# Three blocks of a transformer on one core: in the first two attentions the outputs are scaled instead of the probabilities, and the work around them is dealt out anew

## The reference

```python
# layer 0, per block of 128 queries: 12 heads over the block and 128 keys on either side, and a sink
s = einsum('bqkgd,bskd->bkgqs', q_blk, k_blk) * scale + bias
p = softmax(concatenate([where(valid, s, NEG), sink_l], -1), -1)[..., :SPAN]
o = einsum('bkgqs,bskd->bqkgd', p, v_blk)
# layer 1, per row of a grid 64 wide: 12 heads over all 8 rows and 16 columns around the query
s = einsum('bwhd,brwchd->bhwrc', q_row, k_nb) * scale + bias
o = einsum('bhwrc,brwchd->bwhd', softmax(s), v_nb)
# both: 4 more heads over a memory of 256 tokens
o_mem = einsum('bhsm,bmhd->bshd', softmax(q @ mk * scale), mv)
x = x + rms_norm(concatenate([tok, mem_out], -1) @ w_out[i], g)
```

## Time and profile before

| | |
|---|---|
| time before, median of 3 | 1915.09 us (1914.83 to 1916.83) |
| profiled execution | 1917.37 us, of which the span of the core is 1915.6 us |
| granted clock over the span | 0.997 |
| busy: PE, DVE, ACT, POOL | 1897.8, 964.2, 772.1, 182.8 us |
| windowed phase, scores of turn 4 to the end | 93.57 to 154.74 us of the span |
| grid phase, the same | 681.65 to 739.93 us of the span |

### The profile page before, as it was taken

One profiled execution on the slowest core, in us unless ns is written; L12 is line 12 of the kernel. 1 busy time (PEld: TensorE's weight loads), 2 busy tenths in 40 slices (PEclk: granted clock), 3 DMA queues, 4 the chain that ended last, 5 costly groups with the idle time before them and its releaser, 6 DMA issues.

```text
span 1915.6 us, 25105 instructions
## 1 busy us (share of the span) xinstructions
PE 1897.8 (99%) x10458; PEld 1567.2 (82%) x10458; DVE 964.2 (50%) x1497; ACT 772.1 (40%) x1251; POOL 182.8 (10%) x196
## 2 busy tenths in 40 slices
PE   9999999999999999999999999999999999999998
PEld 7878888888888867888888888878887888888887
DVE  5693665553245284566553236443655555425523
ACT  5494433333333295433333334233764443212321
POOL 4112200000005031300000103000000020000000
PEclk9999999999999999999999999999999999999999
DMA  6512233334333311232233332331112323233222
GB/s 191 197 35 77 80 97 99 99 92 141 93 104 123 99 41 56 89 98 92 97 99 91 102 105 99 99 106 61 59 38 86 116 90 97 99 99 96 93 97 88
DMA packets 54136, 182.96 MB, mean 96 GB/s; under 512 B 6604, under 2 KB 10060, under 8 KB 53512
## 3 DMA queue, kind: packets, MB, share of 16 engines
q1 hardware_dynamic: 51528, 172.28, 28.2%
q0 software_dynamic: 2352, 9.02, 1.6%
q10 hardware_dynamic: 144, 0.06, 0.0%
HBM read 176.58 MB, written 4.76 MB: 95 GB/s over the span
## 4 chain that ended last, share of the span: by engine, by line
PE 88%; ACT 5%; DVE 5%; issue 1%; DMA 1%; SPq 0%; DVEq 0%; ACTq 0%
PE bank L1903 22%; PE bank L1904 22%; PE bank L1905 22%; PE bank L1922 2%; ACT prob_long L848 2%; PE bank L1923 2%; PE bank L1924 2%; ACT pt_short L837 1%; PE bank L2153 1%; PE bank L1683 1%; PE bank L1686 1%; PE bank L1691 1%; PE bank L1981 1%; PE bank L1982 1%; PE bank L1983 1%
## 5 line engine op out<-in xcount | busy, mean ns | idle before, releaser
L1155 DVE TENSOR_TENSOR w_lo<-w_raw,w_hi 128x1024 fp32r<-128x1024 f32 (+3 forms) x319 | 388.6, 1220 | 712.3 <-ACT w_hi L661 711.9
L661 ACT CAST w_hi<-w_raw 128x1024 fp32r<-128x1024 f32 (+3 forms) x319 | 322.0, 1010 | 555.0 <-DMA w_raw<-in_w_down 132.4
L1903 PE MATMUL bank<-h_hi,w_hi 128*128 128x512 f32 x1272 | 497.1, 391 | 0.8 <-DVE w_lo L1155 0.5
L1904 PE MATMUL bank<-h_lo,w_hi 128*128 128x512 f32 x1272 | 496.1, 390 | 0.0
L1905 PE MATMUL bank<-h_hi,w_lo 128*128 128x512 f32 x1272 | 495.9, 390 | 0.0
L1903 PEld LDWEIGHTS bank<-h_hi,w_hi 128*128 128x128 f32 x1272 | 239.5, 188 | 53.1 <-issue 2.2
L1905 PEld LDWEIGHTS bank<-h_hi,w_lo 128*128 128x128 f32 x1272 | 239.5, 188 | 50.2
L1904 PEld LDWEIGHTS bank<-h_lo,w_hi 128*128 128x128 f32 x1272 | 239.5, 188 | 49.5
L1903 PE MATMUL bank<-a_hi,w_hi 128*128 128x512 f32 (+1 forms) x676 | 261.5, 387 | 0.0
L1904 PE MATMUL bank<-a_lo,w_hi 128*128 128x512 f32 (+1 forms) x676 | 261.3, 387 | 0.0
L1905 PE MATMUL bank<-a_hi,w_lo 128*128 128x512 f32 (+1 forms) x676 | 261.3, 386 | 0.0
(11 more groups left out here) (328 smaller groups left out, 2551.6 us busy)
## 6 DMA issues: line engine op xcount, KB each, us to landing
w_raw<-in_w_gu SPq DMA_DIRECT2D x87, 512.0 KB, 3.5
w_raw<-in_w_mlp_in SPq DMA_DIRECT2D x32, 512.0 KB, 3.5
w_raw<-in_w_mlp_out SPq DMA_DIRECT2D x32, 512.0 KB, 3.6
w_raw<-in_w_down SPq DMA_DIRECT2D x32, 448.0 KB, 3.3
w_raw<-in_w_out SPq DMA_DIRECT2D x24, 512.0 KB, 3.6
w_raw<-in_w_down SPq DMA_DIRECT2D x16, 512.0 KB, 3.5
w_raw<-in_w_gates SPq DMA_DIRECT2D x16, 512.0 KB, 3.4
w_raw<-in_w_qk_b SPq DMA_DIRECT2D x14, 512.0 KB, 3.7
```

The source lines that it names most:

```text
L661: nc.scalar.copy(hi_of(v), raw_of(v)).then_inc(w_hi_done, 1)
L1155: nc.vector.tensor_tensor(lo_of(v), raw_of(v), hi_of(v).bitcast(F32), ALU.subtract).then_inc(w_split, 1)
L1903: mm(acc, w1, hi, start=start, stop=False)
L1904: mm(acc, w1, lo, start=False, stop=False)
```

## The change

- **Scaling.** VectorE no longer scales the probabilities. TensorE turns and multiplies the bare exponentials, and so waits for `p_exp` in place of `p_ready`. Once for each pair VectorE takes the reciprocals of all 8 sums and spreads them over 512 columns of `raw` (`spread_roots`); TensorE turns these in 8 more transposes beside those of the next pair's first step (or alone in turn 35), they are copied out with the same `copy_turned` (1024 columns in place of 512), and VectorE multiplies the pair's output by them (`scaled_output`), rounds it and later subtracts (`scaled_remainder`).
- **Skew.** ScalarE makes the exponentials of step `s-1` in turn `s`, no longer those of step `s`.
- **Dealing.** The output operations are VectorE's alone, in different turns of four: the spread in turns 4k+1, the copy of one step's turned probabilities (the pair's last, `by_vector`) in turns 4k+2, the subtraction in 4k+3, the product and rounding in 4k. ScalarE makes three of four copies and no `h_hi`.
- **Ring.** The values of the grid phase lie in a ring of tiles, so that each step reads two whole blocks of 128 key rows; 64 columns of `prob_long` that the first and last query tile don't use are set to zero at the start.
- **Order.** The first dense stage after the attention does seven chunks of its third tile first, and then the last chunks of the first three tiles.

```diff
@@ attention steps of the grid phase
-            spans = [(0, 192, 256, ((0, P), (64, P)), (0, 1), (slice(0, 64), slice(0, P))),
...
+            spans = [(0, 192, 256, 64, (0, 1)), (64, 256, 0, 0, (1, 2)), (192, 256, 0, 0, (2, 3)),
+                     (320, 192, 448, 0, (3, 0))]
@@
+        def turned_blocks(phase, d, steps):
+            begin, end = 0, 2 * len(steps[d].blocks) if d < len(steps) else 4
+            if phase < 2 and d and d % 4 == 0:
+                begin, end = 0 if d < len(steps) else 4, 8
+            return begin, end
+
+        def by_vector(phase, d, steps):
+            return phase < 2 and d < len(steps) and d % 4 == 3
@@ ScalarE, copy_turned and the turn
+                if by_vector(phase, d, steps):
+                    turned[0] += 1
+                    return
...
+                if phase < 2 and d % 4 == 2 and d > 2:
+                    act.wait_ge(o_scaled, scaled[0] + d // 4)
                 act.wait_ge(t_ready, turned[0] + 1)
...
-                        if s < n:
-                            exps(phase, s, steps[s])
-                        if 0 <= s - LAG_V[phase] < n:
-                            copy_output(phase, s - LAG_V[phase], steps, o_hi)
+                        if 0 <= s - 1 < n:
+                            exps(phase, s - 1, steps[s - 1])
@@ VectorE
+                def spread_roots(d):
+                    of = steps[d].pair_no % 2
+                    dve.wait_ge(p_exp, expd[0] + 2 * d + 2)
+                    nc.vector.reciprocal(rden[:, :, :], sums[:, :, :, of]).then_inc(rden_done, 1)
...
+                    nc.vector.tensor_copy(raw[:, of, :].rearrange("p (n d) -> p n d", n=8), spread).then_inc(roots_spread, 1)
+
+                def scaled_output(d):
...
+                    dve.wait_ge(pt_copied, turned[0] + d + 2)
+                    dve.wait_ge(pv_done, pv[0] + d + 1)
+                    nc.vector.tensor_tensor(o, acc, pt_of(phase, d + 1)[:, 4 * P:8 * P], ALU.mult).then_inc(o_scaled, 1)
+                    dve.wait_ge(o_scaled, o_count[0])
+                    nc.vector.tensor_copy(o_hi[:, st.pair, :], o).then_inc(o_hi_done, 1)
...
+                def copy_turned(d):
+                    dve.wait_ge(pv_done, pv[0] + d - 1)
+                    dve.wait_ge(t_ready, turned[0] + d + 1)
...
+                    nc.vector.tensor_copy(dst, src).then_inc(pt_copied, 1)
+
+                def beside_minima(s):
+                    if s >= 5 and s % 4 == 1 and s - 2 < n:
+                        spread_roots(s - 2)
+                    if s >= 8 and s % 4 == 0:
+                        scaled_output(s - 5)
+                        if s >= n:
+                            scaled_remainder(s - 5)
+                    if s >= 11 and s % 4 == 3 and s - 3 < n:
+                        scaled_remainder(s - 8)
+                    if s >= 6 and s % 4 == 2 and s - 3 < n:
+                        copy_turned(s - 3)
@@ VectorE's turn, after the minima of step s
-                        for half in range(2):
-                            part = prob_of(phase, d, half)[:, :steps[d].width]
-                            nc.vector.tensor_scalar(part, part, rden[:, i, half:half + 1], None, ALU.mult).then_inc(p_ready, 1)
...
+                        beside_minima(s)
@@ TensorE, turn
-                    pe.wait_ge(p_ready, ready[0])
+                    pe.wait_ge(p_exp if phase < 2 else p_ready, ready[0])
...
+                if phase < 2 and d and d % 4 == 0:
+                    pe.wait_ge(roots_spread, heads[0] + d // 4)
+                    for i in range(4):
+                        for part in range(2):
+                            last = nc.tensor.transpose(ps[4 + part][:, 256 + 64 * i:256 + 64 * i + 64],
+                                                       raw[rows(part), (d // 4 - 1) % 2, P * i:P * i + P],
+                                                       ident[rows(part), 64 * part:64 * part + 64])
```

More of the change, by code:

```diff
@@ L887, in softmax @@
                 pv[0] += n
-            masked, turned, pv = [0], [0], [0]
+                if phase < 2:
+                    scaled[0] += n // 4
+            masked, turned, pv, scaled = [0], [0], [0], [0]
             logs_and_exps()
@@ L1276, in softmax @@
                 n = len(steps)
+                for i, first in ((0, 0), (3, 192)) if phase == 1 else ():
+                    unused = prob_long[:, 2 * i:2 * i + 2, first:first + 64]
+                    nc.vector.tensor_copy(unused, zero_bias[:, :P].rearrange("p (h k) -> p h k", h=2)).then_inc(round_cleared, 1)
                 if last_values:
@@ L1670, in chunk_order @@
                              for c in range(m)]
+                    if st in w_out:
+                        plain = [(2, 0, c) for c in range(7)] + [(k, 0, 7) for k in range(3)] + plain[3 * DC:]
                     if st is w_out2:
@@ L2058, in turn @@
             def turn(phase, d, steps, act_read):
+                if d == 0 and phase == 1:
+                    pe.wait_ge(round_cleared, 2)
                 if d == 0:
                     wait_reads((act_read, 0, 0))
-                if not 0 <= d < len(steps):
+                if not (0 <= d < len(steps) or phase < 2 and d == len(steps)):
                     return
-                blocks = steps[d].blocks
                 if turned[0]:
                     pe.wait_ge(pt_copied, turned[0])
-                for half in range(2):
+                for half in range(2 if d < len(steps) else 0):
+                    blocks = steps[d].blocks
                     ready[0] += 1
-                    pe.wait_ge(p_ready, ready[0])
+                    pe.wait_ge(p_exp if phase < 2 else p_ready, ready[0])
                     first_key = steps[d].pieces[0][half]["first_key"]
@@ L2083, in softmax @@
                 n = len(steps)
+                if phase == 2:
+                    ready[0] = 0
                 if last_values:
@@ L2134, in softmax @@
                         pe.wait_ge(pt_copied, copied[0])
-                        banks = 1 if phase == 2 else 2
-                        if st.first and st.pair_no >= banks:
-                            pe.wait_ge(o_ready, heads[0] + st.pair_no - banks + 1)
+                        if st.first and phase < 2 and st.pair_no >= 2:
+                            pe.wait_ge(o_scaled, heads[0] + st.pair_no - 1)
+                        elif st.first and phase == 2 and st.pair_no:
+                            pe.wait_ge(o_ready, heads[0] + st.pair_no)
                         n_v = len(st.vs[0])
```

88 lines of the change are left out of this document (48 added, 40 removed).

## The result

| | before | after |
|---|---|---|
| median of 18 executions each | 1915.20 us (1913.61 to 1917.11) | 1920.12 us (1917.67 to 1923.61) |
| ratio | | 1.0023, interval 1.0016 to 1.0031 |
| profiled execution, span | 1917.37, 1915.6 us | 1917.97, 1916.2 us |
| windowed phase, scores of turn 4 to the last product with values | 61.17 us | 64.70 us |
| grid phase, the same | 58.28 us | 58.86 us |

The change makes the kernel slower, by 4.9 us between the medians. The two phases alone, both at full clock, differ by 3.53 + 0.58 = 4.1 us.

The account below looks back on a forecast made before the run. ScalarE and VectorE were nearly full, TensorE's own work within 3% of the bound in the windowed phase. Windowed +3.5 and grid -0.1 gave +3.4 us, so the median 1915.09 becomes 1918.5 us, range 1914.0 to 1922.0.

Parts of the forecast that it names:

- The windowed phase, +3.5: Windowed attention: old waits -3.1, eight transposes 8 x 0.26, new waits +4.2, turn 33 +0.3; sum +3.5 us.
- Wait (a): Turns 4k+2: TensorE waits for VectorE's copy behind both minima; with restart 0.37 us windowed, 0.43 grid, 0.33 at the memory.
- wait (b): Turns 4k+3: TensorE waits for ScalarE's copy of 1024 columns; with restart 0.18 us windowed, 0.28 grid.
- (c): Windowed phase: ScalarE's exponentials of 385 columns between two copies add 0.09 us a pair, between 0 and 0.2.
- The price of VectorE's copy: VectorE's copy of 512 float32 columns out of PSUM: taken as 0.68 us, with 0.42 as the other end.
- The rival of a short copy at 0.42: VectorE's copy takes 0.42 us; 14 waits fall by 0.26 each, -3.6, giving 1914.9, no change; chance 0.12.
- Eight transposes, 0.26: TensorE's eight added transposes for a pair cost 0.26 us on the path, 4.2 us over 16 pairs.
- The rival of hidden copies, -5.9: Copies are hidden and TensorE runs without waits: -5.9 us, giving 1909.2; chance 0.08.
- The grid phase, -0.1: Grid attention: -5.8 old waits, -1.8 64-row products, +2.1 transposes, +4.6 new waits, +0.3 turn 33, +0.5 GpSimd; sum -0.1 us.
- GpSimd's remainder: First grid pairs: VectorE's new operations meet GpSimd's masking and delay VectorE's copy; 0.5 us, ends 0 and 3.
- The rival at +3: GpSimd holds VectorE longer in the first three or four grid pairs: +3 in place of +0.5, giving 1921.0; chance 0.15.
- What was to cost nothing: Skew, VectorE's five new operations outside the priced waits, the last pair's output and the two clears: no cost claimed.

Follow-up runs that it names:

- e1: The changed kernel with VectorE's copy of turned probabilities put ahead of the two minima of its turn; 1913.15 us, ratio 0.9994.
- e5: The kernel before with GpSimd's mask copies for grid pairs 3 to 5 cut to 8 columns; 1912.79 us, ratio 0.9988.
- e6: Windowed attention in the order of the kernel before, grid attention as in e1; 1913.56 us, ratio 0.9994.
- e4: The changed kernel with GpSimd's masks of the bias tables of grid pairs 3 to 5 added on 8 columns only; 1919.17 us, ratio 1.0019.
- e8: e2 with the skew taken back, exponentials of step s in turn s again; 1915.03 us, ratio 0.9999.
- e2: The changed kernel with ScalarE making all four copies of a pair, VectorE none; 1914.97 us, ratio 1.0000.
- e3: The changed kernel without the 8 transposes of spread reciprocals in all turns but each phase's last; 1915.61 us, ratio 1.0004.
- e7: As e6, but ScalarE makes all four copies of a grid pair; 1913.10 us, ratio 0.9988.
- e9: The kernel before with the third block's 16 single-column products dealt one column at a time behind 8 projection chunks; 1913.61 us, ratio 0.9993.
- e10: e7 with the same edit as e9, narrow products dealt behind projection chunks; 1911.10 us, ratio 0.9978.

## Why the prediction was right, and where it was off

The forecast was 1918.5 us, in a range of 1914 to 1922; the runs gave 1920.12, inside. The chance for slower by over 0.2% was 0.40, that for no change 0.49, and the ratio, 1.0023, is just over the bound: what happened was not what the prediction held likeliest of the three. Of the 1.5 us between forecast and median, 0.7 is in the phases, all of it in the grid phase; the rest lies outside them. The direction, the place and the price were worked out before the run; by its steps:

- *The windowed phase, +3.5*: measured +3.53. Wait (a), forecast 0.37 with restart, measured 0.34; wait (b), forecast 0.18, measured 0.13; (c), forecast 0.09, measured 0.04 before one transpose and 0.05 before another. The period was forecast at 7.8 and is 7.87.
- *The price of VectorE's copy*, unknown from the trace of before: 0.68 was taken, 686 ns measured. The rival of a short copy at 0.42 falls. By the Trainium skill, "VectorE: DVE Perf Modes", section "Why PSUM operands drop a tier", a float32 operand in PSUM takes away VectorE's faster modes, and the estimate from that page was 0.66 us; this trace agrees with 0.686 (and with 0.427 for the copy of 512 columns that stays in SBUF).
- *Eight transposes, 0.26*: measured 0.27 by leaving them out.
- *The rival of hidden copies, -5.9*: did not come, and for the reason given: order, not load. Even e1, which takes the order away, comes, in the two phases, to 5.6 under the change and only 1.5 under the kernel before, as waits of 2.1 and 2.8 remain.
- *The grid phase, -0.1*: measured +0.58. The step that failed is that the sum takes off all old waits, 5.76. One of them is at the start of the phase, in turn 4, and stays:

```profile
684.71 0.60 PE L2177 MATMUL bank<-k_buf,q_buf 64*128 64x192 f32 x4 [0.39 <-DVE low_stat L1374]
685.27 0.60 ACT L851 ACTIVATE pt_short<-bank 128x512 f32<-128x512 f32 x1
...
685.92 0.46 PE L2134 MATMUL bank<-ident,prob_long 64*128 64x64 f32 x8 [0.61 <-ACT pt_short L851]
```

  The distance from the scores to the transposes is 1.21 where 0.43 is bare, 0.78 of wait; before it was 0.88. ScalarE reads the last values and makes the first exponentials ahead of that copy in both kernels. With this one term the sum would have been +0.7. No run takes this wait away, so that it explains the difference is read from the trace alone.
- *GpSimd's remainder, 0.5 of between 0 and 3*: measured 0.35. The rival at +3 falls. The reading of the earlier trace rows, that GpSimd makes the difference between the waits of the two phases, 2.7 us, holds for 2.3 of it (e5). By distances the grid phase of e6 is 2.6 under that of before from three terms: 1.8 less for the ring (12 groups at 0.59 in place of 0.74), 2.1 more for the transposes, and waits of 2.8 in place of 5.76. Of these 2.9 us of waits, 2.3 are those that e5 loses without any output scaling. So scaling the outputs alone would bring the grid phase some 0.8 us, and mostly because VectorE is no longer so busy while GpSimd works. The ring was not run by itself.
- *What was to cost nothing*: from the windowed phase's end to the grid phase the changed kernel needs 526.37 us and e5, which has neither clears nor ring, 526.33; from the grid phase's end to the third block's scores 510.01 and 509.95. In these two executions the two clears, the new order and the last pair's output cost nothing. Between the phases other kernels need 526.3 to 527.7 by one profile each, so less than that spread can't be told.
- *The execution profiled*: the 2.3 us by which before's stood over its median were subtracted from the forecast, which was right to do, though the reason was not known then: the profiled execution carries the larger fall of the clock, 3.2 us, and most executions a smaller one (24 of the 33 of the kernel before beside e1 to e4 have a mean clock of 0.998).

The whole in its parts, by stretch, from the kernels that differ in one of them:

| us | windowed | grid | from |
|---|---|---|---|
| outputs scaled, four copies on ScalarE; in the grid phase also the ring | +1.38 | -2.41 | e8 less before |
| the skew | -0.24 | -0.25 | e2 less e8 |
| the fourth copy on VectorE, behind the minima | +2.39 | +3.24 | after less e2 |
| the change | +3.53 | +0.58 | |

Scaling the outputs loses in the windowed phase: eight transposes a pair add 2.1 us, and waits that were only 3.1 fall to about 2. In the grid phase it wins 0.8, since the waits were twice as long; the other 1.8 is the ring's, by which the products over 64 rows go. The copy on VectorE loses in both, by its place behind the minima: ahead of them (e1) it costs nothing. The third block, unchanged, gave and took next to nothing from its scores to the end, 662.4 us before and 662.6 after.

Partly open: why the medians of e2 and e8 stand 1.4 above what their phases give. Two things outside the phases vary, the clock's fall (0, 1.6 or 3.2 us) and a wait of TensorE for ScalarE's squares between the first two layers, here of e8_no_skew, by the waits of TensorE in 554 to 608 us:

```profile
PE bank L2066 <- ACT sq L709: 1.2, 1, 1.2
```

It is 0.8 in e1's profile, 0.4 in that of before, and none in e2's and the change's. In e8 it makes the way from phase to phase 0.8 longer than before (527.73 against 526.91), which with the phases, -1.03, gives the -0.3 of its executions at 0.999. In e2 those agree with the phases, so the excess of its median lies in the executions with a lower clock. Both rest on two executions each, and why a kernel falls longer or more often was not shown. Not tried: the ring without output scaling, and a split of the copy between both engines.

## What to carry to other kernels

Unloading an engine gains only what the bound engine waited for: add up these waits by distances first (8.9 us here), and hold against them what the change puts on the bound engine (4.2 us) and each handover that it delays. An instruction that frees a buffer which exists once belongs ahead of work that itself waits for a later product of the engine that needs the buffer; one line's place was worth 5.6 us. And where two attentions share code, ask for each by itself: in its better order (e1) the scheme lost 1.15 us in the windowed one and gained 2.6 in the grid one, and of these 1.8 came from the ring and 0.8 from the scaling.

## What the runs showed of the hardware

- TensorE's granted clock fell to half within or just behind a run of 16 products of one column each, which takes 2.55 us, although TensorE's busy share was 10.00 of 10.00 us before, during and after. Of the ten profiles it fell at this place in five; it cost 1.6 us in e3, e7 and e8 and 3.2 in before and e1. The Trainium skill, "TensorE: Matmul & The Clock Gate", section "What's actually happening", says that the gate follows how busy TensorE has been; the busy share here does not show it, the dealing of the narrow products does (e9, e10: 19 of 22 executions at 0.999).
- A mean clock of 0.999 or 0.998 tells executions of one kernel apart: of the kernel before beside e9, 4 at 0.999 have a median of 1914.06 and 16 at 0.998 one of 1915.55.
- How much GpSimd's masks lengthen VectorE's work depends on what VectorE does meanwhile: the same masks cost the kernel before 2.30 us of the path and the changed one 0.35. The rounding of 512 columns takes 428 ns in the windowed phase and 585 in the mean of the grid phase, where the two beside GpSimd's first masks take 0.92 and 0.87 us. The copy out of PSUM takes 686 and 684. The prediction counted the subtraction among what GpSimd holds up; at 704.66, with GpSimd at work throughout, it took 0.68, no more than elsewhere (0.69).

```profile
L1338 DVE COPY pt_short<-bank 128x512 f32<-128x512 f32 x8 | 5.5, 684 | 0.0
...
L1324 DVE CAST h_hi<-act_out 128x512 fp32r<-128x512 f32 x7 | 4.1, 585 | 0.2
```
